# Row sums of a gated mixer halved ahead of a product with ones, and a key mask spread by DMA instead of by a product

## What is computed

```python
def layer_norm(x, g, b):                       # mixer B, over 256 features
    xc = xf - jnp.mean(xf, axis=-1, keepdims=True)
    var = jnp.mean(xc * xc, axis=-1, keepdims=True)
    return xc * lax.rsqrt(var + EPS) * g + b
...
_, idx = lax.top_k(score, n_sel)               # mixer A
logits = jnp.einsum('bqhd,bqkhd->bhqk', q, k_sel) * HEAD_DIM ** -0.5
p = jax.nn.softmax(jnp.where(valid, logits, -inf))
```

## Time and profile before

| What | Value |
|---|---|
| median of three runs | 1100.61 us |
| the profiled execution, its own time | 1100.77 us |
| span of its trace (first to last instruction) | 1099.0 us |
| PE busy | 1070.9 us (97%) |
| PE weight loads busy | 979.9 us (89%) |
| POOL, ACT, DVE busy | 699.9, 601.3, 574.0 us (64%, 55%, 52%) |
| the 16 DMA engines, share on SP's queue | 55.4% |

### The profile page before, as it was taken

One profiled execution on the slowest core, in us unless ns is written; L12 is line 12 of the kernel. 1 busy time (PEld: TensorE's weight loads), 2 busy tenths in 40 slices (PEclk: granted clock), 3 DMA queues, 4 the chain that ended last, 5 costly groups with the idle time before them and its releaser, 6 DMA issues.

```text
span 1099.0 us, 22903 instructions
## 1 busy us (share of the span) xinstructions
PE 1070.9 (97%) x8188; PEld 979.9 (89%) x8188; DVE 574.0 (52%) x1363; ACT 601.3 (55%) x1112; POOL 699.9 (64%) x319
## 2 busy tenths in 40 slices
PE   5999999999999999999999999999999999999996
PEld 2887788898899999999998777889899999999996
DVE  4557743555267755553247576344626685555112
ACT  3564456445446665655456545554545776656542
POOL 0874545445567887778877444545557788777882
PEclk9999999999999999999999999999999999999999
DMA  9955467766654454445566546774534435444541
GB/s 358 362 212 197 186 231 281 235 232 227 199 180 159 148 183 163 153 165 180 191 210 246 209 177 229 252 255 155 189 119 154 154 132 185 176 157 153 191 166 73
DMA packets 85694, 214.95 MB, mean 196 GB/s; under 512 B 13336, under 2 KB 33376, under 8 KB 85360
## 3 DMA queue, kind: packets, MB, share of 16 engines
q1 hardware_dynamic: 85616, 213.88, 55.4%
HBM read 208.80 MB, written 5.05 MB: 195 GB/s over the span
## 4 chain that ended last, share of the span: by engine, by line
PE 85%; DVE 10%; ACT 2%; DMA 2%; issue 1%; SPq 1%; DVEq 0%; POOL 0%; ACTq 0%
PE ps L720 11%; PE ps L716 11%; PE ps L717 11%; PE ps L755 10%; PE ps L756 9%; PE ps L757 9%; PE ps L652 4%; PE ps L708 2%; PE ps L707 2%; PE ps L706 2%; PE ps L1120 2%; PE ps L646 1%; DVE scr L1770 1%; DVE hup L1690 1%; PE ps L861 1%
## 5 line engine op out<-in xcount | busy, mean ns | idle before, releaser
L596 POOL TENSOR_TENSOR wlo<-raw,whi 128x1024 fp32r<-128x1024 f32 x282 | 675.6, 2401 | 347.9 <-ACT whi L1214 290.0
L1214 ACT ACTIVATE whi<-raw 128x1024 fp32r<-128x1024 f32 x202 | 211.6, 1054 | 83.2 <-PE ps L720 62.6
L755 PE MATMUL ps<-hh,whi 128*128 128x288 f32 x816 | 250.6, 307 | 0.8 <-ACT gb L1296 0.8
L756 PE MATMUL ps<-hl,whi 128*128 128x288 f32 x816 | 241.6, 296 | 0.0
L757 PE MATMUL ps<-hh,wlo 128*128 128x288 f32 x816 | 241.3, 296 | 0.0
L755 PEld LDWEIGHTS ps<-hh,whi 128*128 128x128 f32 x816 | 153.7, 188 | 39.0 <-issue 36.2
L717 PE MATMUL ps<-ol,whi 128*128 128x290 f32 x576 | 156.9, 297 | 0.0
L716 PE MATMUL ps<-oh,whi 128*128 128x290 f32 x576 | 156.7, 297 | 0.0
L756 PEld LDWEIGHTS ps<-hl,whi 128*128 128x128 f32 x816 | 153.9, 189 | 0.2
L757 PEld LDWEIGHTS ps<-hh,wlo 128*128 128x128 f32 x816 | 153.7, 188 | 0.0
L716 PEld LDWEIGHTS ps<-oh,whi 128*128 128x128 f32 x576 | 108.9, 189 | 0.0
(11 more groups left out here) (264 smaller groups left out, 1907.0 us busy)
## 6 DMA issues: line engine op xcount, KB each, us to landing
raw<-stream SPq DMA_DIRECT2D x228, 512.0 KB, 4.2
mraw<-stream SPq DMA_DIRECT2D x40, 1024.0 KB
raw<-stream SPq DMA_DIRECT2D x88, 128.0 KB, 5.0
raw<-stream SPq DMA_DIRECT2D x24, 384.0 KB, 5.4
first<-mod_first SPq DMA_DIRECT2D x16, 512.0 KB, 11.6
raw<-stream SPq DMA_DIRECT2D x28, 256.0 KB, 5.2
o_proj<-proj SPq DMA_DIRECT2D x12, 288.0 KB
kvk<-keys_t SPq DMA_DIRECT2D x6, 512.0 KB, 6.4
```

The source lines that it names most:

```text
L596: nc.gpsimd.tensor_tensor(wlo[:, slot, :], raw[:, slot, :], whi[:, slot, :].bitcast(F32), ALU.subtract).then_inc(lo_ready, 1)
L755: mm(out, whi[:, slot, w], high, start=(i == 0), stop=False)
L756: mm(out, whi[:, slot, w], low, start=False, stop=False)
L1214: A(whi[:, slot, :], raw[:, slot, :], ACT.Copy).then_inc(hi_ready, 1)
```

## The change

Five things are changed.

- `b_mean`: DVE adds the two halves into `scr` in slot 9 (signal `rows_added`), and PE multiplies ones by the one sum.
- `b_var`: ACT squares the halves in two operations, the first into PSUM bank 7, the second into `scr`; DVE adds them in slot 12 (`squares_paired`), and PE has one product.
- `sample_logits`: the two products with the repeating matrix and PE's wait for `chosen` go; the heads' logits start their own sums.
- SP copies the mask four times, onto partitions 0, 32, 64 and 96 of `fl8` (free by then), four DMAs of 32 x 544 behind the load of the piece six after that of slot 46, once `chosen` is signalled. DVE adds this to the sample logits in `greatest`, waiting for the copies.
- The last round of `choose` and the making of the mask move from slot 47 to slot 45.

```diff
@@ sync engine @@
+                    if q == piece_at(46) + 6:
+                        sp.wait_ge(pv_done, upto(l, pv_done, 8))
+                        sp.wait_ge(chosen, upto(l, chosen, 3))
+                        for h in range(NH):
+                            sp.dma_start(sample_mask[h * TS:(h + 1) * TS, :], score[0:TS, 3 * P:]).then_inc(mask_spread, 16)
@@ tensor engine @@
-                    pe.wait_ge(gelued, upto(l, gelued))
-                    for j in range(2):
-                        i = mm(ps[:, 7, 0:T], cst[:, C_ONE:C_ONE + P], proj[:, BV + j, :], start=(j == 0), stop=(j == 1))
-                    i.then_inc(mean_ready, 1)
+                    pe.wait_ge(rows_added, upto(l, rows_added))
+                    mm(ps[:, 7, 0:T], cst[:, C_ONE:C_ONE + P], scr[:, 0, :], start=True, stop=True).then_inc(mean_ready, 1)
...
-                    pe.wait_ge(centred_squared, upto(l, centred_squared))
-                    for j in range(2):
-                        i = mm(ps[:, 7, 0:T], cst[:, C_ONE:C_ONE + P], scr[:, j, :], start=(j == 0), stop=(j == 1))
-                    i.then_inc(var_ready, 1)
+                    pe.wait_ge(squares_paired, upto(l, squares_paired))
+                    mm(ps[:, 7, 0:T], cst[:, C_ONE:C_ONE + P], scr[:, 0, :], start=True, stop=True).then_inc(var_ready, 1)
...
-                        pe.sem_inc(settled, 1)
-                        pe.wait_ge(chosen, upto(l, chosen, 3))
-                        rep = cst[0:TS, C_REP:C_REP + P]
-                        mm(ps[:, 2, :], rep, score[0:TS, 3 * P:3 * P + PAST], start=True, stop=False, **kw)
-                        mm(ps[:, 3, 0:TS], rep, score[0:TS, 3 * P + PAST:3 * P + PAST + TS], start=True, stop=False, **kw)
@@ scalar engine @@
-                        A(scr[:], proj[:, BV:BV + 2, :], ACT.Square).then_inc(centred_squared, 1)
+                        A(ps[:, 7, 0:T], proj[:, BV, :], ACT.Square)
+                        A(scr[:, 1, :], proj[:, BV + 1, :], ACT.Square).then_inc(centred_squared, 1)
@@ vector engine @@
+                            in_order(V.tensor_tensor(lg, lg, sample_mask, ALU.add))
...
-                last_rounds = {32: 1, 33: 2, 35: 2, 37: 2, 39: 1, 40: 2, 41: 2, 43: 2, 45: 2, 47: 1}
+                last_rounds = {32: 1, 33: 2, 35: 2, 37: 2, 39: 1, 40: 2, 41: 2, 43: 2, 45: 3}
...
+                    if t == 9:
+                        dve.wait_ge(gelued, upto(l, gelued))
+                        V.tensor_tensor(scr[:, 0, :], proj[:, BV, :], proj[:, BV + 1, :], ALU.add).then_inc(rows_added, 1)
+                    if t == 12:
+                        dve.wait_ge(centred_squared, upto(l, centred_squared))
+                        V.tensor_tensor(scr[:, 0, :], ps[:, 7, 0:T], scr[:, 1, :], ALU.add).then_inc(squares_paired, 1)
```

More of the change, by code:

```diff
@@ L269, in encoder @@
         fl8 = scratch("fl8", [P, 2, T])
+        sample_mask = fl8[:].rearrange("p j n -> p (j n)")[:, 0:PAST + TS]
         fcum = scratch("fcum", [P, TP + PAST + TS])[0:8]
@@ L356, in encoder @@
         mean_ready = signal("mean_ready", 1)
+        rows_added = signal("rows_added", 1)
+        squares_paired = signal("squares_paired", 1)
+        mask_spread = signal("mask_spread", 4 * 16)
         centred = signal("centred", 1)
@@ L881, in sample_logits @@
                         pe.wait_ge(kv_a_loaded, upto(l, kv_a_loaded))
-                        pe.sem_inc(settled, 1)
-                        pe.wait_ge(chosen, upto(l, chosen, 3))
-                        rep = cst[0:TS, C_REP:C_REP + P]
-                        mm(ps[:, 2, :], rep, score[0:TS, 3 * P:3 * P + PAST], start=True, stop=False, **kw)
-                        mm(ps[:, 3, 0:TS], rep, score[0:TS, 3 * P + PAST:3 * P + PAST + TS], start=True, stop=False, **kw)
                     for h in range(NH):
-                        mm(ps[TS * h:TS * (h + 1), 2, :], queries[:, h, :], kvk[:, h // 2, :], start=(n != A_ROWS), stop=(n != C_ROWS), **kw)
+                        mm(ps[TS * h:TS * (h + 1), 2, :], queries[:, h, :], kvk[:, h // 2, :], start=True, stop=(n != C_ROWS), **kw)
                     for h in range(NH):
-                        i = mm(ps[TS * h:TS * (h + 1), 3, 0:TS], queries[:, h, :], proj[:, k_t + h // 2, TP:T], start=(n != A_ROWS),
+                        i = mm(ps[TS * h:TS * (h + 1), 3, 0:TS], queries[:, h, :], proj[:, k_t + h // 2, TP:T], start=True,
                                stop=(n != C_ROWS), **kw)
@@ L1863, in greatest @@
                     if n == A_ROWS:
-                        dve.wait_ge(chosen, upto(l, chosen, c + 1))
+                        if c < 2:
+                            dve.wait_ge(chosen, upto(l, chosen, c + 1))
+                        else:
+                            dve.wait_ge(mask_spread, upto(l, mask_spread))
                     dve.wait_ge(logits, upto(l, logits, 3 * n + c + 1))
@@ L2096, in _ @@
                     if t in last_rounds:
-                        choose(2, last_rounds[t], t == 47)
+                        choose(2, last_rounds[t], t == 45)
                     if l + 1 < DEPTH:
```

## The result

The changed kernel takes **1106.05 us** (median of 10 executions, 1103.36 to 1110.5) against 1100.62 us for the kernel before beside it (10 executions, 1099.63 to 1101.74): a ratio of 1.0050, 95% interval 1.0037 to 1.0062. The forecast was 1099.6 us, the range 1096.3 to 1101.5. Even the fastest execution lies above the range.

A forecast was written before the change was run, and what follows sets the result against it. PE was taken as the bound, busy 1070.9 of 1099.0 us. Gains of 1.92 and 2.39 us less a loss of 3.32 gave 1.0 us gained, 1099.6 us; range 1096.3 to 1101.5.

The forecast's parts named there:

- Part 1: Row sums of mixer B (`b_mean`, `b_var`, two layers): one product of two records less each, 4 x 0.48 = 1.92 us gained.
- The rival that swallows this gain: Mixer B's gain lost in the chain ending in the 1.2 us waits: 1.92 us lost, 1101.5 us; chance 0.04.
- the swap product's 1.2 us wait: PE's wait for DVE at slot 18, one per layer, largest inside the mixers; assumed unable to swallow mixer B's gain.
- Part 2: Mask of mixer A: the two products with the repeating matrix go altogether, 1.20 + 1.19 = 2.39 us gained.
- Part 3, the chain: Slots 45 to 47: moved round and mask delay `greatest`, `exps` and `take_gate`, so PE waits at slot 47's gate tile.
- Part 3, the price of the wait: Slot 47: DVE's added 2.1 us becomes PE waits of 1.45 and 1.87 us by layer, 3.32 us lost.
- the question of lockout: Slot 9: whether DVE's addition with two SBUF inputs waits for POOL; forecast one wait, done about 69.3, nothing on the path.
- The sum: Whole kernel: 1.92 + 2.39 - 3.32 = 1.0 us gained, giving 1099.6 us.
- The slower rival: Mask copies land late, slot 48's addition waits and PE waits at slot 49: 1102.8 us; chance 0.07.
- The rival "finds room": DVE, ACT or PE make up the moved round's 2.1 us before slot 47: 4.3 us gained, 1096.3 us; chance 0.26.

## Why the prediction was wrong

By its own steps:

- **Part 1** was right as a local cost (1.17 to 0.69 us, four times) and in the time as far as the runs can tell: 1.7 us measured, between 0.2 and 2.1, where 1.92 were summed. The additions were hidden. The rival that swallows this gain was named at the wrong place: not the swap product's 1.2 us wait, but slot 43 of the second layer, where in one execution a weight load came only 0.33 us earlier when PE came 1.48 us earlier.
- **Part 2** was right: 1.72 to 0.53 us on PE in the trace, and 2.5 us between the medians of the moved round with and without the mask's new way, for 2.39; that the medians fit so well is luck.
- **Part 3, the chain**, was right link by link: PE waits at the gate tile of slot 47 for `take_gate`, in both layers, and nowhere for the mask.
- **Part 3, the price of the wait: mis-sized.** Its 2.1 us took 0.43 for the making of the mask from a row of slot 47. It measured 0.90 and 1.21. The waits came to 1.84 + 2.81 - 0.22 = 4.43 us for 3.32. This could have been read: in the trace of before POOL is in two operations just where the step was to go.

```profile
254.23 4.74 POOL L596 TENSOR_TENSOR wlo<-raw,whi 128x1024 fp32r<-128x1024 f32 x2 [1.67 <-ACT whi L1214]
254.25 0.47 DVE L1932 TENSOR_TENSOR ps<-ps,gb 128x288 f32<-128x288 f32 x1
```

  The round would begin at 254.25 and the mask at 254.25 + 1.66 = 255.91; the first of POOL's two ends at 254.23 + 2.37 = 256.60, 0.7 us later. The prediction asked the question of lockout for the addition with two inputs from SBUF, and not for this operation with one. The Trainium skill, "SBUF — State Buffer", section "Who interferes with whom", names `tensor_scalar` among those that can take the port pair that VectorE shares with GpSimd, under conditions on its operands. The trace agrees, with 0.42 or 0.43 us where POOL is idle or comes second and 0.74 to 1.24 us in the seven profiles where POOL came first.
- **The sum: a term was missing.** Each wait was charged its own length, and a lower clock behind it was put at nothing, without a reason. In three of four profiles it came at one or both waits and cost 1.5 or 2.7 us each, 2.5 us an execution on average. With the measured waits the sum is -4.31 + 4.43 = +0.1 us, about the kernel before; with the clock +2.6, that is 1103.2. The changed kernel's medians are 1106.05 and, measured again, 1103.83. Most of what lies between these two is clock: 7.0 us of it are missing on average in the first ten executions, 5.0 in the twelve later ones. Three of the first ten (1107.77 to 1110.5) are about 2 us above all other executions of this kernel even with their missing clock taken off; the profiled one with the long start is among them, and the cause of the other two is open.
- **The range** failed with it: every rival charged a wait of PE at its length, so none reached above 1101.5 by the mechanism that was forecast. The slower rival was put on the mask's copies, which never were late.
- **The rival "finds room"** was not so in slot 45, but it was in slot 42: there one round costs PE no wait at slot 47 beyond the old one, and the time is 1097.2.

## What to carry to other kernels

Where PE is the bound and streams, price a new wait as its length plus what the clock may take behind it, and put that into the range: here 4.4 us of waits brought about 2.5 us more, in some executions and not in others. Before an operation of VectorE is moved, look at what GpSimd does at the place it moves to, not only at what the operation took at the place it left. And when two gains are paid for by one moved step, look for another slot for that step first: the idle time of its engine (2.76 us in slot 42) was worth 6.6 us here (1103.83 to 1097.25), more than the two gains together, 4.3.

## What was not expected of the hardware

- The granted clock fell to 0.50 in or behind waits of 1.84 and 2.81 us inside an otherwise full stretch (five times of eight), and once some 2 us behind one of 1.17; it stayed down 3.4 us or twice that though PE was busy again. A product then began every 0.24 us instead of every 0.13. In another execution the same waits left it at 1.00, and so did all four waits that were filled with dummy products: eight dummy products, 1.72 + 2.69 = 4.4 us in the trace, took 2.1 us off the time of one kernel and 3.8 off the other's.
- A VectorE operation with two inputs from SBUF took 7.59 us instead of 0.44, through several GpSimd operations that followed each other, not one.
- An operation of VectorE with one input from SBUF, 0.43 us by itself, ended 0.3 us after a GpSimd operation that had begun ahead of it, and took 0.74 to 1.24 us.
